# A two-layer diffusion backbone in split fp32 on one core: weight split in two pieces, low-half products behind the high-half ones, spreads and two modulation sums at later places

## The reference, cut to what matters

```python
for i in range(DEPTH):                                  # DEPTH = 2
    m = split(silu(c) @ w_mod[i] + b_mod[i], 9)         # shift, scale, gate, three times
    h = h + 0.5 * m[2] * swiglu(modulate(rms_norm(h), m[0], m[1]), w_ff_in[i, 0], w_ff_out[i, 0])
    a = modulate(rms_norm(h), m[3], m[4])
    y = fourier_mix(a, ...) if i == 0 else conformer_conv(a, ...)
    h = h + m[5] * y
    h = h + 0.5 * m[8] * swiglu(modulate(rms_norm(h), m[6], m[7]), w_ff_in[i, 1], w_ff_out[i, 1])
# swiglu(h, w_in, w_out): g, u = split(h @ w_in, 2); return (silu(g) * u) @ w_out    (inner width 2816)
# modulate(h, shift, scale): return h * (1 + scale) + shift
```

## Time and profile before

| | us |
|---|---|
| median of 3 runs | 1922.47 |
| lowest and highest | 1920.95, 1924.53 |
| the profiled execution | 1923.38 |
| its span | 1921.6 |
| TensorE busy in it | 1833.9 (95%) |
| mean granted clock of TensorE | 0.98 |

### The profile page before, as it was taken

One profiled execution on the slowest core, in us unless ns is written; L12 is line 12 of the kernel. 1 busy time (PEld: TensorE's weight loads), 2 busy tenths in 40 slices (PEclk: granted clock), 3 DMA queues, 4 the chain that ended last, 5 costly groups with the idle time before them and its releaser, 6 DMA issues.

```text
span 1921.6 us, 21937 instructions
## 1 busy us (share of the span) xinstructions
PE 1833.9 (95%) x8540; PEld 1501.1 (78%) x8540; DVE 1202.8 (63%) x1531; ACT 621.4 (32%) x787; POOL 163.5 (9%) x145
## 2 busy tenths in 40 slices
PE   5899999999989999999999999999995999999999
PEld 2788888877877888888888888888772698888888
DVE  6867676766878767666774444447688454545354
...
DMA packets 160536, 239.09 MB, mean 124 GB/s; under 512 B 3821, under 2 KB 110525, under 8 KB 160220
## 3 DMA queue, kind: packets, MB, share of 16 engines
...
## 4 chain that ended last, share of the span: by engine, by line
PE 77%; DVE 12%; ACT 4%; POOL 3%; issue 2%; DMA 2%; SPq 0%; POOLq 0%; DVEq 0%; ACTq 0%
PE bank L1563 14%; PE bank L1565 14%; PE bank L1570 14%; PE bank L1456 10%; PE bank L1457 10%; PE bank L1458 10%; DVE bank L1409 3%; DVE mod_acc L953 2%; POOL tmp_c L586 2%; DVE w_lo L930 2%; PE bank L1537 1%; PE bank L1532 1%; PE bank L1530 1%; DMA raw_pair<-in_w_mod 1%; POOL sq_sum L551 1%
## 5 line engine op out<-in xcount | busy, mean ns | idle before, releaser
L1563 PE MATMUL bank<-a_hi,w_hi 128*128 128x512 f32 x1408 | 551.5, 392 | 4.7 <-ACT a_hi L634 4.7
L1565 PE MATMUL bank<-a_hi,w_lo 128*128 128x512 f32 x1408 | 548.8, 390 | 0.0
L1570 PE MATMUL bank<-a_lo,w_hi 128*128 128x512 f32 x1408 | 434.4, 390 | 1.5 <-DVE a_lo L1025 1.5
L1563 PEld LDWEIGHTS bank<-a_hi,w_hi 128*128 128x128 f32 x1408 | 264.8, 188 | 61.6 <-issue 6.3
L1140 DVE SCALAR_TENSOR_TENSOR h<-bank,half_gate,h 128x512 f32<-128x512 f32 x320 | 234.2, 747 | 122.9 <-PE bank L1458 121.9
L1570 PEld LDWEIGHTS bank<-a_lo,w_hi 128*128 128x128 f32 x1408 | 264.6, 188 | 57.5 <-DVE a_lo L1025 2.5
L1565 PEld LDWEIGHTS bank<-a_hi,w_lo 128*128 128x128 f32 x1408 | 264.9, 188 | 56.3 <-issue 1.4
L1456 PE MATMUL bank<-p_hi,w_hi 128*128 128x512 f32 (+1 forms) x768 | 287.4, 374 | 6.6 <-DVE h L1147 3.8
L1457 PE MATMUL bank<-p_hi,w_lo 128*128 128x512 f32 (+1 forms) x768 | 286.0, 372 | 0.0
L1458 PE MATMUL bank<-p_lo,w_hi 128*128 128x512 f32 (+1 forms) x768 | 285.9, 372 | 0.0
L930 DVE TENSOR_TENSOR w_lo<-raw_pair,w_hi 128x2048 fp32r<-128x2048 f32 x106 | 245.8, 2319 | 62.6 <-ACT w_hi L745 47.9
...
## 6 DMA issues: line engine op xcount, KB each, us to landing
...
```

The source lines that it names most:

```text
L1563: pe.matmul(ps[banks + s][:], tile_hi, a_hi[:, k], start=k == 0, stop=False, skip_group_check=True)
L1565: pe.matmul(ps[banks + s][:], tile_lo, a_hi[:, k], start=False, stop=False, skip_group_check=True)
L1570: ins = pe.matmul(ps[banks + s][:], w_hi[b][:, s * KD + k], a_lo[:, k], start=False, stop=k == KD - 1, skip_group_check=True)
```

## The change

Six edits, all of order or of where a wait stands; no product is added or taken away.

1. `in_half`, for the first chunk over half 0: the 32 products with `a_hi` of all 8 k come first and the 16 with `a_lo` behind them. `half_sums` of half 1 moves from behind k = 2 to behind the high products of k = 4, `half_spread` of half 1 from behind k = 5 to behind the whole chunk.
2. VectorE's order in the norms: `half_lo` of k = 0 to 3 no longer stands between the `half_normed` and `flush_half` of k = 0 to 3, but behind them; with k = 4 to 7 `half_lo(k-4)` and `half_normed(k)` alternate, and `half_rstd` of half 1 comes ahead of the last four `half_lo`.
3. The 128x2048 weight split ahead of norms 1, 3 and 4 is done in two pieces of 128x1024, the first behind 2 `flush_half`, the second behind 5 (before: the whole behind 4).
4. `half_spread` of half 0 in `project` moves from in front of the last group to behind its first three matmuls.
5. The sums of units u0-2 and u0-1 move from in front of `up(f, 1, 0)` and `up(f, 1, 1)` to the middle (behind k = 3) of those chunks.
6. VectorE's `mod_columns(1)` and `half_gate` in step 1 move behind the weight split of chunk 0; for feed-forward 0 `down` waits for the columns at d = 2.

```diff
             def ff_norm(n, layer, v, call, next_lo_unit, among=None):
                 f = NORM_FF[n]
-                for d in range(4):
+                flush_half(f, 0, 0)
+                flush_half(f, 0, 1)
+                next_lo_unit(0)
+                for d in range(2, 5):
                     flush_half(f, 0, d)
-                next_lo_unit()
-                for d in range(4, KD):
+                next_lo_unit(1)
+                for d in range(5, KD):
                     flush_half(f, 0, d)
...
                 for k in range(4):
                     half_normed(n, 0, k, layer, v)
                     flush_half(f, 1, 4 + k)
-                    if k > 0:
-                        half_lo(n, 0, k - 1, layer, v)
                 if among is None:
-                    half_normed(n, 0, 4, layer, v)
-                    half_lo(n, 0, 3, layer, v)
-                    for k in range(5, KD):
-                        half_normed(n, 0, k, layer, v)
-                        half_lo(n, 0, k - 1, layer, v)
-                    half_lo(n, 0, KD - 1, layer, v)
+                    for k in range(4):
+                        half_lo(n, 0, k, layer, v)
+                        half_normed(n, 0, 4 + k, layer, v)
                     half_rstd(n, 1)
+                    for k in range(4, KD):
+                        half_lo(n, 0, k, layer, v)
                     half_chunks(n, 1, range(KD), layer, v)
                     return
+                for k in range(3):
+                    half_lo(n, 0, k, layer, v)
                 half_lo(n, 0, 3, layer, v)
...
             def ff_step(f, i, par, unit, last_step, next_unit, after_down):
                 down_lo((DOWN[f][0], i + (DOWN[f][1] - 1)))
-                if after_down is not None:
-                    after_down()
+                if after_down is not None and FF_UNIT0[f] is not None:
+                    mod_row(FF_UNIT0[f] - 1)
                 if unit is not None:
                     mod_mac(unit, mod_half_ready(i * 16 + 16 * (FF_UNIT0[f] - HEAD + 2)), ring_rows)
...
+                if after_down is not None:
+                    after_down()
                 gated(f, i, 1, par)
...
             def in_half(b, banks, n, hf, waits_a):
+                lo_apart = waits_a and hf == 0
...
+                    if lo_apart:
+                        if k == 4:
+                            half_sums(n, 1)
+                        continue
...
-                    if waits_a and hf == 0 and k == 2:
-                        half_sums(n, 1)
-                    if waits_a and hf == 0 and k == 5:
-                        half_spread(n, 1)
+                if lo_apart:
+                    for k in range(KD):
+                        pe.wait_ge(s_half_a[hf], KD * r + k + 1)
+                        for s in range(2):
+                            pe.matmul(ps[banks + s][:, hs], w_hi[b][:, s * KD + k], a_lo[:, k, hs], start=False,
+                                      stop=k == KD - 1, skip_group_check=True)
+                    half_spread(n, 1)
+                    return None
...
             def in_chunk(b, banks, waits_a, done, mid_unit=None):
...
+                    if k == 3 and mid_unit is not None:
+                        pe.wait_ge(s_mod_row, mid_unit)
+                        mod_sum(mid_unit)
...
             def down(f, done, par, unit, columns=None):
...
+                    if d == 2 and columns is not None:
+                        pe.wait_ge(s_mod, columns)
...
                 def step(i, par, late_unit=False):
-                    up(f, i, 0, False)
-                    if late_unit:
-                        pe.wait_ge(s_mod_row, u0 - 1)
-                        mod_sum(u0 - 1)
-                        if f == 0:
-                            mod_transpose(1)
-                    up(f, i, 1, False)
+                    up(f, i, 0, False, u0 - 2 if late_unit else None)
+                    up(f, i, 1, False, u0 - 1 if late_unit else None)
+                    if late_unit and f == 0:
+                        mod_transpose(1)
```

45 lines of the change are left out of this document (25 added, 20 removed).

## The result

| | before | after |
|---|---|---|
| median of 7 runs, us | 1922.47 | 1927.66 |
| lowest and highest | 1920.95, 1924.53 | 1926.03, 1931.32 |
| ratio, 95% interval | 1 | 1.0027 (1.0017 to 1.0037) |
| the profiled execution, its span | 1923.38, 1921.6 | 1927.66, 1925.9 |

The change makes the kernel 5.2 us slower by the medians and 4.3 us by the spans of the profiled executions. Forecast were 1927.1 us and +4.65.

A forecast was written before the change was run, and what follows sets the result against it. TensorE, busy in 95% of the span, was taken as the bound. The terms 3.7 + 2.9 - 1.3 - 0.6 + 0.6 + 0.5 - 1.15 gave +4.65 us on the 1922.47 median: 1927.1 us, range 1921.5 to 1931.0.

The forecast's parts named there:

- feed-forward 0: Step 1: the sum of u0-1 comes later than VectorE needs it, so d = 3 starts late, +3.7 us.
- feed-forward 1: Step 1: same late sum, d = 3 starts at 623.4 instead of 620.52, +2.9 us.
- feed-forward 2: Step 1: no unit accumulated, so the 1.59 us wait at 983.45 goes, -1.3 us.
- norms 3 and 4: High products first: chunk 0 over half 0 ends earlier, -0.3 us each, -0.6 in all.
- norm 1: Four more VectorE instructions stand ahead of the first Fourier product; its block of 12 products comes +0.6 us later.
- norm 6: Spread behind three matmuls: 0.5 us later, but the clock drop behind 1.91 us of idle goes, -1.15 us.
- I leave that drop where it was: Feed-forward 1, step 1: clock 0.50 for 3.3 us behind the idle at 620.52, costing 1.65 us, assumed to stay.
- rival (b): Feed-forward 1: idle time splits, clock drop falls on matmuls that wait anyway, -1.65, 1925.4 us; chance 0.22.
- Rival (c): More clock loss: drops in feed-forward 0's longer idle stretches, norm 6 keeps its drop, 1928.8 to 1930.5 us; chance 0.18.
- the neighbour wait: VectorE: waiting for the instruction directly in front costs about 0.13 us; four such waits per norm.
- rival (d): Neighbour wait costs nothing: norms 3, 4, 2 and 6 each gain 0.5 more, 1925.0 us, not slower; chance 0.12.
- Weight split: Two pieces in norms 1, 3, 4: sums still wait for GpSimd's last addition, 0 to -0.2 us each, taken as 0.

The follow-up runs named there:

- e2: Kernel before with edits 5 and 6 alone (moved sums, columns and `half_gate`), norms as before: 1926.90 us, ratio 1.0026.
- e3: Changed kernel, but the sum of u0-1 stands behind k = 0 instead of k = 3: 1921.78 us, ratio 0.9997 to the kernel before.
- e5: Kernel before with edits 5 and 6, the sum of u0-1 behind k = 0, no norm edits: 1919.39 us, ratio 0.9995.
- e10: Kernel before with edits 1 and 2 in norms 3 and 4 alone, in the change's own order: 1920.48 us, ratio 0.9985.
- e9: Kernel before with edit 2 in norm 1 alone (`half_lo` behind all `flush_half`): 1924.81 us, ratio 1.0013.
- e1: Changed kernel with edits 5 and 6 taken back, so edits 1 to 4 alone: 1924.68 us, ratio 1.0011 to the kernel before.
- e4: Changed kernel, but the sum of u0-1 stands behind k = 5 instead of k = 3: 1934.65 us, ratio 1.0063 to the kernel before.
- e6: Kernel before with edit 3 alone (weight split in two pieces): 1924.10 us, ratio 1.0014.
- e7: Kernel before with edits 1 and 2 in norms 3 and 4 alone, VectorE reordered so no `half_normed` waits for the `half_lo` in front: 1926.56 us, ratio 1.0035.
- e8: Kernel before with edit 4 alone (spread of half 0 in norms 2 and 6 behind three matmuls): 1919.85 us, ratio 0.9994.

## Why the prediction was right, and where its terms were off

The time and the direction were right: +4.65 forecast, +5.2 by the medians, +4.3 in the trace. By its steps:

| term | predicted | in the trace of after | in traces where the clock gave nothing back |
|---|---|---|---|
| feed-forward 0 | +3.7 | +3.7 | +3.7 (e2) |
| feed-forward 1 | +2.9 | +1.3 | +2.9 (e2) |
| feed-forward 2 | -1.3 | -1.2 | -1.2 (e2, e3, e5) |
| norms 3 and 4 | -0.6 | +0.3 | -0.6 (e10) |
| norm 1 | +0.6 | +0.6 | first product +1.2 (e9); the whole norm not shown |
| norm 2 | +0.5 | +1.7 | +0.4 to +0.7 (e1, e3, e4) |
| norm 6 | -1.15 | -1.1 | as predicted (e1, e3, e4) |
| ahead of step 1; the convolution | 0, 0 | +0.3, -1.3 | 0, 0 |

**Feed-forward 0 and 2** are right in size and in mechanism: the chain of VectorE behind a late sum. The sum and the update were forecast at 93.06 and 93.77; they came at 93.38 and 94.04 with 0.3 us of drift. The slope of one was shown by e4, the corner by e3.

**Feed-forward 1** was mis-sized by the step "I leave that drop where it was". d = 3 came 2.94 us later, as forecast, but the drop came 0.3 us behind the start of u0's sum (621.45), after that sum's new wait of 2.82 us, and none came behind d = 3. That is rival (b) in its place, with another reason: I had asked whether the second idle stretch was under 1.6 us, and it was 1.88. The step that failed was to tie the drop to the wait at d = 3 alone. In e2, with the same code in this step, both drops came, so whether the second one comes is not settled by the order.

**Rival (c)** had its condition too: a drop came in step 1 of feed-forward 0, which I had named as a sign of being wrong. It cost nothing, since d = 2 and d = 3 still waited for VectorE behind it. My other sign, d = 3 not later by 3 us, was met in feed-forward 1 by 0.06 us (2.94). And what I held against it, that the 2.01 us at 90.25 had no drop, was weak: five of the kernels that keep this wait (e1, e6, e7, e8, e10) have a drop right behind it, +0.9 us, and the two traces of before and e9 have none.

**Norms 3 and 4**: the structure was right to the tenth, and so was the neighbour wait. The pairs of 0.91 us (0.39 and 0.52) show it against rival (d): where a wait for the instruction in front stands, 0.13 us are lost. The Trainium skill (page "VectorE: DVE Perf Modes", section "The DRAIN you can't avoid") says that the pipe is emptied behind every instruction and that the semaphore costs nothing on top, and adds that a next instruction which is not held starts earlier. By these rows the independent neighbour starts 0.39 us behind a 0.48 us instruction and the dependent one 0.52, so here the wait costs 0.13 us, and the measurement decides. What the prediction lacked is the clock: a drop in one of the two norms in the trace, which turned -0.6 into +0.3.

**Weight split**: right in place and cause as to the start of the sums (0.05 us later in norm 3, 0.0 in norm 1 of e6). The Trainium skill (page "SBUF — State Buffer", section "Who interferes with whom") says that a VectorE instruction with two inputs from SBUF contends with a GpSimd instruction that reads SBUF. The trace agrees, with additions of 1.19 and 1.73 us instead of 0.73 beside the pieces. What I did not ask is what the longer wait ahead of the sums does to the clock; e6, 3.0 us slower by the medians, leaves that open.

**Norm 1** failed in a step that looked harmless: "less 0.4 us that this `half_lo` lost beside GpSimd; the second `a_lo` follows 0.4 behind instead of 1.2". The first did lose its collision, but the second took it over (433.82, two in 1.34 us), so the second product came no earlier and the whole 1.2 us stayed. With the longer wait came a drop at the product, which I had not in the sum either. In the trace both were covered, since the two drops that the kernel before has later in norm 1 were gone. e9 has the same wait and drop and is 1.4 us slower by the medians; how much of the 1.2 us reaches the end of the norm at equal clock no trace shows.

**Norm 6** is right in size. That the drop was certain with 1.9 us of idle and gone with 1.55 was more than the rows bore out, as e2, e5 and e10 show.

So the sum was near for two reasons: the two large terms were right, and among the small ones an unforeseen +1.2 (norm 2), +0.9 (norms 3 and 4) and -1.3 (convolution), all by the clock, met -1.6 in feed-forward 1. The first is understanding, the second is luck.
